# A position bias turned by DMA, and an output bias added by VectorE

## The reference

```
proj = x @ w_in[l]
a_glu, q, k, v, q_idx, k_idx, w_idx = jnp.split(proj, SPLITS, axis=-1)
conv_out = conv_group(a_glu, ...)                 # GLU, causal conv(31), LN, silu
# attention, one block of 128 queries:
score = jnp.einsum('bths,bth->bts', relu(q_idx . k_idx), w_idx)
_, sel = lax.top_k(causal score, 64)
dist = q_pos - sel
logits = q . k[sel] * scale + rel_bias[rel_bucket(dist)]
att_out = softmax(logits) @ v[sel]
mix = jnp.concatenate([conv_out, att_out], axis=-1) @ w_out[l] + b_out[l]
x = layer_norm(ALPHA * x + mix, ln1_g[l], ln1_b[l])
y = peer(x, ...)                                  # 128 rows of u_tab and of v_tab per token
x = layer_norm(ALPHA * x + y, ln2_g[l], ln2_b[l])
```

## Time and profile before

| what | value |
|---|---|
| median of 3 runs | 1866.46 us (1864.16 to 1868.92) |
| the profiled execution: its time | 1864.74 us |
| its span | 1862.8 us |
| busy PE, DVE, POOL, ACT | 81%, 64%, 44%, 16% |
| DMA queues, 640 us to the end | full, about 420 GB/s |

### The profile page before, as it was taken

One profiled execution on the slowest core, in us unless ns is written; L12 is line 12 of the kernel. 1 busy time (PEld: TensorE's weight loads), 2 busy tenths in 40 slices (PEclk: granted clock), 3 DMA queues, 4 the chain that ended last, 5 costly groups with the idle time before them and its releaser, 6 DMA issues.

```text
span 1862.8 us, 17122 instructions
## 1 busy us (share of the span) xinstructions
PE 1511.3 (81%) x5812; PEld 907.7 (49%) x5812; DVE 1188.7 (64%) x2028; ACT 303.7 (16%) x428; POOL 823.1 (44%) x681
## 2 busy tenths in 40 slices
PE   8999999999996868767777766887766777876777
PEld 7899799877993323323333322333322333322333
DVE  4699998545699765756646575744655444555445
ACT  4533354534331000000000000000000000000000
POOL 0000000003884756556555555465456555556552
PEclk9999999999996989888888888898888888887889
DMA  7355443454557899999999999999999999999996
GB/s 267 136 181 185 177 149 126 163 197 180 200 192 308 336 423 422 422 422 422 421 422 422 421 421 422 408 423 422 422 422 422 422 422 422 422 422 422 421 422 276
DMA packets 91101, 633.76 MB, mean 340 GB/s; under 512 B 10354, under 2 KB 13106, under 8 KB 14642
## 3 DMA queue, kind: packets, MB, share of 16 engines
q0 software_dynamic: 74464, 542.16, 70.3%
q1 hardware_dynamic: 13828, 88.76, 13.1%
q10 hardware_dynamic: 2768, 2.33, 0.4%
HBM read 631.08 MB, written 2.12 MB: 340 GB/s over the span
## 4 chain that ended last, share of the span: by engine, by line
PE 42%; DMA 29%; DVE 18%; issue 5%; POOL 4%; ACT 1%; POOLq 0%; SPq 0%; DVEq 0%; ACTq 0%
PE psum L659 27%; DMA v_row<-in_v_tab,eslot_v 23%; DMA u_row<-in_u_tab,eslot_u 5%; PE psum L414 4%; PE psum L415 4%; PE psum L416 4%; DVE scratch L990 4%; DVE w_lo L935 3%; POOL v_row L342 2%; DVE u_row L1233 2%; POOL u_row L342 1%; DVE scratch L1185 1%; PE psum L537 1%; DVE scratch L1156 1%; DVE scratch L1200 1%
## 5 line engine op out<-in xcount | busy, mean ns | idle before, releaser
L659 PE MATMUL psum<-v_row,scratch 128*128 128x512 f32 x2032 | 945.7, 629 | 314.1 <-DMA v_row<-in_v_tab,eslot_v 227.6
L1233 DVE CUSTOM_DVE_ANT_0 u_row<-u_row,x 128x2048 f32<-128x2048 f32 x256 | 585.0, 2308 | 513.9 <-DMA u_row<-in_u_tab,eslot_u 507.3
L659 PEld LDWEIGHTS psum<-v_row,scratch 128*128 128x128 f32 x2032 | 408.2, 203 | 851.9 <-issue 569.9
L342 POOL DMA_INDIRECT v_row<-in_v_tab,eslot_v x256 | 404.2, 1579 | 113.7 <-issue 61.8
L342 POOL DMA_INDIRECT u_row<-in_u_tab,eslot_u x248 | 263.2, 1061 | 108.5 <-issue 58.0
L414 PE MATMUL psum<-xT_hi,w_hi 128*128 128x256 f32 x896 | 258.3, 288 | 10.1 <-POOL w_lo L307 4.8
L415 PE MATMUL psum<-xT_lo,w_hi 128*128 128x256 f32 x896 | 254.8, 284 | 0.0
L416 PE MATMUL psum<-xT_hi,w_lo 128*128 128x256 f32 x896 | 254.6, 284 | 0.0
L884 ACT ACTIVATE gel<-dots 128x4 f32<-128x4 f32 x64 | 13.1, 205 | 1187.4 <-DVE dots L1233 1164.9
L414 PEld LDWEIGHTS psum<-xT_hi,w_hi 128*128 128x128 f32 x896 | 173.0, 193 | 14.1 <-issue 7.9
L415 PEld LDWEIGHTS psum<-xT_lo,w_hi 128*128 128x128 f32 x896 | 173.2, 193 | 0.3 <-issue 0.2
(11 more groups left out here) (184 smaller groups left out, 905.4 us busy)
## 6 DMA issues: line engine op xcount, KB each, us to landing
w_raw<-in_w_stream SPq DMA_DIRECT2D x80, 1024.0 KB, 4.8
v_row<-in_v_tab,eslot_v POOLq DMA_INDIRECT x256, 20.9
u_row<-in_u_tab,eslot_u POOLq DMA_INDIRECT x248, 21.7
xT_raw<-in_xT SPq DMA_DIRECT2D x4, 512.0 KB, 6.5
skew<-dist_rows ACTq DMA_DIRECT2D x1, 2048.0 KB, 11.3
x<-in_x_tok POOLq DMA_DIRECT2D x1, 2048.0 KB, 10.1
ln_rows_sb<-in_ln_rows POOLq DMA_DIRECT2D x2, 1024.0 KB, 8.3
out_dram<-x SPq DMA_DIRECT2D x8, 256.0 KB, 4.7
```

The lines of the kernel that those rows point to most:

```text
L342: pool.indirect_dma_start(dst, None, tab, bass.IndirectOffsetOnAxis(ap=ids, axis=0)).then_inc(land, 16)
L659: last = pe.matmul(ps[4 * i + n][:, :], diag[k][:, j, :], v_ring[k * G + j][:, n * 512:(n + 1) * 512], start=False, stop=True, skip_group_ ...
L1233: return dve.tensor_tensor_reduce(u_ring[s], u_ring[s], x1[:, i, :], 1.0, 0.0, ALU.mult, ALU.add, dst)
```

## The change

The rows of the bias are turned by a DMA. POOL, behind the index stage (`w_used` at 8), stores `dist_row` to DRAM 128 times, each copy shifted by minus one element (2 MB in pieces of 1 KB, read from the 16 partitions of `dist_row`), waits for that to land, and loads the result as `bias` (2 MB in pieces of 1 KB). Both stand ahead of its two `cut`s. The eight products by `flip`, the eight copies by ACT, the store and the load that ACT issued, and `flip` itself are gone; DVE waits for the load (`bias_in`) where it waited for the copies. For the output, POOL loads b_out into all 128 partitions (`b_all`, 1 MB in place of 8 KB), DVE forms ALPHA * x + b_all once for each half of the tokens, and adds the bank to it; the products with ones are gone, and the last product of a unit raises `mix_done`.

```diff
+            pool.wait_ge(w_used, U_GLU)
+            pool.wait_ge(row_copied, 1)
+            pool.dma_start(turned_rows, bass.AP(tensor=dist_row, offset=P - 1, ap=[[SKEW, NH], [-1, P], [1, S]])).then_inc(row_out, 16)
+            pool.wait_ge(row_out, 16)
+            pool.wait_ge(x_split, 4)
+            pool.dma_start(bias, turned_rows.rearrange("h p s -> p h s")).then_inc(bias_in, 16)
+
             cut(scored, acc, FILL)
             cut(masked, mask, NEG)
 
             pool.wait_ge(w_used, U_OUT)
-            pool.dma_start(b_row, b_out).then_inc(b_in, 16)
+            pool.dma_start(b_all, b_out.to_broadcast([P, D])).then_inc(b_in, 16)
...
-            pe.wait_ge(skew_in, 16)
-            pe.wait_ge(pool_const, 2)
-            for n in range(8):
-                pe.wait_ge(bias_copied, max(n - 1, 0))
-                pe.matmul(ps[6 + n % 2][:, :], flip[:, :], skew[:, 2 * n:2 * n + 2, :].rearrange("p h s -> p (h s)"),
-                          start=True, stop=True).then_inc(flip_done, 1)
...
                     for i in tiles:
                         last = exact(ps[bank + i], [t[:, 4 * q + c, i * P:(i + 1) * P] for t in (cat_h, cat_l)],
-                                     [t[:, c, :] for t in w], m + c == 0, False)
+                                     [t[:, c, :] for t in w], m + c == 0, m + c == 6)
+                        if m + c == 6 and i == 0:
+                            last.then_inc(mix_done, 1)
...
-                    pe.matmul(ps[bank + i], ones_row[:, :], b_row[:, n * 512:(n + 1) * 512], start=False, stop=True).then_inc(mix_done, 1)
...
-            act.wait_ge(row_copied, 1)
-            act.dma_start(row_scratch, dist_row[:, :]).then_inc(row_out, 16)
...
-                if u == 2:
-                    act.wait_ge(row_out, 16)
-                    act.dma_start(skew, bass.AP(tensor=row_scratch.tensor, offset=0, ap=[[1, P], [SKEW, NH], [1, S]])).then_inc(skew_in, 16)
...
-            for n in range(8):
-                act.wait_ge(flip_done, n + 1)
-                act.activation(bias[:, 2 * n:2 * n + 2, :].rearrange("p h s -> p (h s)"), ps[6 + n % 2][:, :], ACT.Copy).then_inc(bias_copied, 1)
...
-                    dve.wait_ge(bias_copied, 8)
+                    dve.wait_ge(bias_in, 16)
...
                 if n == 0:
                     dve.wait_ge(row_in, 16)
+                    dve.wait_ge(b_in, 16)
+                    for i in range(TI):
+                        last = dve.scalar_tensor_tensor(out=x1[:, i, :], in0=x1[:, i, :], scalar=ALPHA, in1=b_all,
+                                                        op0=ALU.mult, op1=ALU.add)
+                    link(last)
                 for i in range(TI):
                     x_n = x1[:, i, n * 512:(n + 1) * 512]
-                    dve.wait_ge(mix_done, TI * n + i + 1)
-                    dve.scalar_tensor_tensor(out=x_n, in0=x_n, scalar=ALPHA, in1=ps[(6 if n % 2 else 0) + i][:, :],
-                                             op0=ALU.mult, op1=ALU.add).then_inc(mix_read, 1)
+                    if i == 0:
+                        dve.wait_ge(mix_done, n + 1)
+                    else:
+                        dve.wait_ge(w_used, U_OUT + RING * (n + 1))
+                    dve.tensor_tensor(x_n, x_n, ps[(6 if n % 2 else 0) + i][:, :], ALU.add).then_inc(mix_read, 1)
```

More of the change, by code:

```diff
@@ L98, in layer @@
         xl = put("xT_lo", "x_lo", [P, KC, S], F32R)
-        b_row = put("b_row", "x_hi", [1, D])
+        b_all = put("b_all", "x_hi", [P, D])
         w_raw = [put(f"w_raw{k}", "w_lo", [P, UNIT], plus=8 * k) for k in range(RING)]
@@ L108, in layer @@
         x1c = [put(f"x1T_chunks{k}", "bias", [P, 2 * S], plus=8 + 2 * k) for k in range(4)]
-        skew = put("skew", "cat_hi", [P, NH, S])
         h_most = put("glu_sb", "cat_hi", [P, CC - 1, TAPS - 1 + S])
@@ L142, in layer @@
         ident_a = sb("ident_alpha", [P, P])
-        flip = sb("flip", [P, P])
         mean_w = sb("mean_w", [P, P])
@@ L210, in layer @@
         diag = [tmp("peer", G * P).rearrange("p (j t) -> p j t", j=G) for k in range(RG)]
-        row_scratch = nc.dram_tensor("dist_rows", (NH, SKEW), F32, kind="Internal").ap()
+        turned_rows = nc.dram_tensor("turned_rows", (NH, P, S), F32, kind="Internal").ap()
         x_split = sem("x_split")
@@ L225, in layer @@
         w_in = [sem(f"w_in{k}") for k in range(RING)]
-        row_out, skew_in = sem("row_out"), sem("skew_in")
+        row_out, bias_in = sem("row_out"), sem("bias_in")
         out_done = sem("out_done")
@@ L234, in layer @@
         qidx_copied, score_done, relu_done, idx_added = (sem(n) for n in ("qidx_copied", "score_done", "relu_done", "idx_added"))
-        row_done, row_copied, flip_done, bias_copied = (sem(n) for n in ("row_done", "row_copied", "flip_done", "bias_copied"))
+        row_done, row_copied = sem("row_done"), sem("row_copied")
         scored, masked = sem("scored"), sem("masked")
@@ L291, in _ @@
             pool.memset(ident_a[:, :], 0.0)
-            pool.memset(flip[:, :], 0.0)
             pool.memset(mean_w[:, :], 1.0 / DC)
@@ L300, in _ @@
             pool.affine_select(out=ident_a[:, :], in_=ident_a[:, :], compare_op=ALU.not_equal, fill=ALPHA,
-                               base=0, pattern=[[-1, P]], channel_multiplier=1)
-            pool.affine_select(out=flip[:, :], in_=flip[:, :], compare_op=ALU.not_equal, fill=1.0,
-                               base=-(P - 1), pattern=[[1, P]], channel_multiplier=1).then_inc(pool_const, 1)
+                               base=0, pattern=[[-1, P]], channel_multiplier=1).then_inc(pool_const, 1)
             def lower(n, u, k):
@@ L484, in _ @@
                     if k == 3:
-                        pe.wait_ge(bias_copied, 8)
+                        pe.wait_ge(row_copied, 1)
                     for half in range(2):
@@ L606, in _ @@
             for n in range(4):
-                bank = 6 if n % 2 else 0
                 pe.wait_ge(mix_read, max(n - 1, 0) * TI)
@@ L613, in _ @@
                         mix(n, m)
-                pe.wait_ge(b_in, 16)
-                for i in range(TI):
-                    if n == 3:
+                if n == 3:
+                    for i in range(TI):
                         mix(n, RING - 1, (i,))
-                    pe.matmul(ps[bank + i], ones_row[:, :], b_row[:, n * 512:(n + 1) * 512], start=False, stop=True).then_inc(mix_done, 1)
             for m in range(KC // 2):
@@ L1009, in _ @@
                 if j == 2:
-                    dve.wait_ge(flip_done, 8)
                     dve.memset(h_most[:, :, 0:TAPS - 1], 0.0)
```

## The result

The changed kernel takes 1871.14 us in the median (1867.91 to 1873.48, 20 runs); the kernel before, run beside it, 1867.19 us (1862.05 to 1870.02, 20 runs). The ratio is 1.0024 with a 95% interval of 1.0017 to 1.0031, which is +4.5 us (3.2 to 5.8): a small loss, inside the 0.3% that the prediction calls no change; it said 1869.4. The profiled execution has a span of 1868.2 us, 5.4 more than before.

The account below looks back on a forecast made before the run. The bound was taken as DVE from 95 us, PE from 376 to 450, DMA queues from 640. 22.9 + 2.8 - 22.8 = +2.9 us on 1864.7 gives 1867.6; the median, 1.7 higher, 1869.4; range 1855 to 1880.

Parts of the forecast that it names:

- What bounds the kernel: First part: PE up to 81 us, DVE from 95, with 1.2 us of weight waits to 345; DMA queues from 640.
- The output products: Output stage, 376 to 450 us: dropping the products with ones gains 8.65 us (bounds 7.85 and 8.65).
- The cover of the wide pair: Output stage: DVE's two wide instructions, 4.6 us, are hidden before PE needs unit 54, with 1.8 us to spare.
- The flip: Behind the index scores: without the eight flip products PE reaches unit 8 6.3 us earlier, DVE's unit 12 at most that.
- The added wait: POOL's cuts wait for store and load: DVE's unit 12 is later by X + g - 14.15, the kernel by X + g - 22.8.
- X: Time from the 2 MB store's issue at 72.3 us to its landing: 22.9 us, bounds 11.3 and 55.7.
- g: Time that issuing the load of 2048 pieces holds POOL: 2.8 us, bounds 0.6 and 5.8.
- DVE's wait covers them: Three weight loads, 4.8 us each in the median, fall into the store's time and were claimed hidden by DVE's wait.
- The second rival: The store is slower than taken: X 30.4, g 5.8, +13.4 us, 1879.9; slower from X + g = 28.4; chance 0.23.
- The pause of PE: Between units 10 and 11 PE pauses 11 us and loses about 3 us to its clock; nothing counted.
- The first: Rival: the narrow source costs the store little, X 11.3, g 2.8; -8.7 us, 1857.8; chance 0.28.
- The third: Rival: PE bounds behind 95 us, so a late DVE costs nothing; gain 8.65 us, 1857.8; chance 0.04.

Follow-up runs that it names:

- the kernel with the DRAM source and the early copy: The changed kernel with the 16 rows first stored to DRAM, and POOL's 2 MB copy reading them there, issued near 20 us: 1854.04 us, ratio 0.9934 to before.
- the kernel that reads every eighth partition: The changed kernel with each head's row held by eight partitions, the store reading every eighth of 128: 1860.94 us, ratio 0.9973 to the kernel before.
- the two experiments that missed: The changed kernel with the first cut ahead of both DMAs, 1867.62 us, or with the store issued near 20 us, 1861.11 us; 1852 to 1854 expected of each.
- the DRAM source: The changed kernel with the 16 rows first stored to DRAM (24 KB, by ACT), where POOL's 2 MB store reads them: 1857.21 us, ratio 0.9959 to before.
- cut first: The changed kernel with POOL's first cut written ahead of its two DMAs, the source still 16 partitions: 1867.62 us, ratio 1.0010 to the kernel before.
- the wide source: POOL's 2 MB store reading the rows from DRAM; here the changed kernel with that and the first cut ahead of both DMAs: 1855.52 us, ratio 0.9946.
- the other four experiments: The kernel before with the output part alone (1857.12 us) or position part alone (1880.84); the changed kernel with first cut ahead (1867.62) or store near 20 us (1861.11).

## Why the prediction was right, and where it was not

**What bounds the kernel.** Right. The tail is untouched, DVE has nothing in which to catch up: its +14.3 at unit 13 is still +14.2 at 320 us (320.93 before, 335.14 after, the lowering behind the same convolution step).

**The output products.** 8.65 us taken, 8.4 measured in the kernel with that part alone (interval 6.0 to 10.8); by the trace of that kernel the normalisation behind the last block starts 8.47 earlier (444.08 instead of 452.55). The bounds were 7.85 and 8.65. The cover of the wide pair held, and the blocks lie 2.1 us closer: DVE's second and third reads are 21.8 us apart (410.58 and 432.34), where they were 23.9 apart (401.20 and 425.10).

**The flip.** Its 6.3 us were called the most that the stage can gain. With the wait gone, in the kernel with the DRAM source and the early copy, DVE is 4.15 us earlier at unit 12 (4.7 without the late start of that execution, 0.55 at unit 9). The 6.3 came from the side of PE and ACT alone. DVE's own list sets the rest, from the same timeline:

```profile
80.28 2.33 DVE L921 TENSOR_TENSOR w_lo<-w_raw,w_hi 128x2048 fp32r<-128x2048 f32 x1 [0.32 <-DVE scratch L938]
82.90 0.62 DVE L952 MAX8 best<-scratch 128x8 f32<-128x128 f32 x2 [0.29 <-POOL scratch L310]
```

Unit 10 begins when the scores are added up, and from there to 90.85 DVE has work, with 0.3 us of idle time. The step did not ask whether DVE could use what PE and ACT had gained.

**The added wait.** The formula, a change of X + g - 22.8, gives 25.8 + 1.2 - 22.8 = +4.2 with the measured values; measured +4.5. Its part for DVE, X + g - 14.15, gives 12.9; the trace has 14.3, of which 0.7 is a late start of the whole profiled execution (unit 9 lowered at 76.37 instead of 75.68).

**X.** 22.9 taken, 25.8 measured, between the bounds of 11.3 and 55.7. The middle by ratio came close, but had no mechanism behind it. That mechanism was there to weigh: the page's 20 us was nearer than the dist_rows row, whose one piece for each engine showed nothing of it. The reason for the upper bound, that each partition gives only its share, falls with the kernel that reads every eighth partition: 16 partitions, 13.9 us.

**g.** 2.8 taken by the slope of the earlier trace rows, 1.21 measured, and 1.24 for the first issue. 2048 pieces hold POOL 1.7 times as long as 256 did (0.73), and by the slope it would have been four times. The errors in X and g have opposite signs, +2.9 and -1.6, so the sum came out 1.3 us short of what the formula gives with the measured values. That it was so near is in part this luck.

**"DVE's wait covers them."** This sentence on the weight loads was the wrong step. It took 4.8 us each for them, from a row of loads with the engines to themselves. In the event they were starved until the store ended. In the changed kernel DVE's wait did cover them, so the time came out; but as an account of what the position part costs the step is wrong, and it led straight to the two experiments that missed. The second rival had the loads beside the store as a reason for a larger X, not as a victim.

**The pause of PE.** Cuts expected near 98, begun at 100.65; a gap of DVE of some 17, found 18.6; unit 11 done at 103.7, found 106.5 (104.21 + 2.29); unit 12 near 106, found 109.29. The three times are 2.7 us late together; 1.3 of that is X + g (27.0 for 25.7), 0.7 the late start, and the rest lies between the steps: POOL issues 0.3 later still, and goes on 0.3 behind the landing. Behind the gap the granted clock was at the lower level. Windows of the changed kernel, columns as in the earlier trace rows:

```profile
92.00:104.00 12.00, 1.40 (x12) 1.19 (x10) 2.56 (x12) 2.76 (x2) 1.86 (x3) 0.74 0.98 287
104.00:110.00 6.00, 3.44 (x16) 3.44 (x17) 5.83 (x15) 1.06 (x1) 0.00 (x0) 0.50 1.01 359
110.00:116.00 6.00, 6.00 (x47) 6.00 (x47) 5.75 (x17) 1.29 (x2) 0.00 (x0) 0.89 0.13 36
```

PE's pause is the 13.2 us of the waits view, where 11 were expected: it is done with unit 10 at 93.4 and starts again at 106.56, when unit 11 is lowered. There it is granted 0.50, the lower of the two levels (1.2 GHz of 2.4), up to 111; from 112 on it has 1.00. DVE is busy for 5.83 of the six us from 104 on: it did not wait for the slow PE, so nothing was to be counted, as said.

**The rivals.** The first (a narrow source costs little) falls with X = 25.8. What it said of a store of 11.3 us, 1857.8, is what the DRAM source gave with 11.0: 1857.2. That the match is so close is partly chance, since its g was 1.6 too large and 1.5 us are lost later, to PE's clock (last section). The third (the delay is absorbed) falls with the constant shift. The second was the right kind (the store is slower than taken), but short of its point of decision: X + g was 27.0, and it needed 28.4.

## What to carry to other kernels

Before a transfer is put beside a stream, look at which partitions it reads: one that reads from 16 neighbouring partitions kept the DMA engines 96% busy at 121 GB/s, where they move 420 in the last part of this kernel, and the other loads paid, at each of the three places tried. When a wait is long, ask what else ends with it: taking one cause away shows the next (cut first: 18.6 us for POOL became 14.1 for the weights), so a test that removes the wait alone does not measure its price. And a delay passes through a bound engine in full: 14.3 us late stayed 14.2. A lead needs a second look: 4.2 us early became 2.7, by a fall of PE's clock that a kernel without a lead had as well.

## What the runs showed of the hardware

**The narrow store and the other queue.** From 78 to 98 us the weight queue got 63 packets to the store's 481 (the DMA view of the changed kernel, above), though three loads were issued. The Trainium skill, DMA: Bandwidth & Descriptors, "Queues, rings and completion order", says that a DMA engine takes turns between its queues by whole packets. A load of 1 MB is 144 packets in the view (288 for two in the same stretch of the kernel before). With a turn for each packet of the store, some 24 in a microsecond, the loads issued at 82.1 and 87.8 would have been through by 98. The trace does not agree, as far as the profile's packets are those that the page means, which no view tells. With the wide source (325 to 527) it is much nearer. Why the narrow store gets so much more than its turns, no run here shows.

**POOL and DVE.** A small DVE instruction waits while POOL subtracts. DVE's timeline of the changed kernel, and POOL's:

```profile
454.33 1.25 DVE L1074 SCALAR_TENSOR_TENSOR minus_mean_rstd<-mv,rstd 128x1 f32<-128x1 f32 x1
```

```profile
450.98 4.58 POOL L302 TENSOR_TENSOR w_lo<-w_raw,w_hi 128x2048 fp32r<-128x2048 f32 x1 [0.98 <-ACT w_hi L704]
```

The same instruction took 0.16 us before; now its end falls together with that of POOL's, at 455.56. The other way round stands above: POOL's cut took 2.69 us beside DVE's lowering. The Trainium skill, SBUF — State Buffer, "Who interferes with whom", has the rule: the two share a pair of ports as an exclusive lock, which counts when POOL reads SBUF beside a DVE instruction with two SBUF inputs. Both rows agree. How much of that 1.1 us reaches the end was not tried.

**1.5 us lost to PE's clock.** In all three kernels with the DRAM source DVE is ahead of the kernel before by a constant amount up to the lowering near 313 us, and by 1.5 us less at the next. The waits of the early one (70 to 345 us) name the place, and before it was 2.2 us:

```profile
DVE convT L1042 <- PE psum L548: 3.7, 1, 3.7
```

The kernel with every eighth partition, which has no lead there (DVE 0.3 us late at 314 us), loses the same 1.5 us. What these four share, and the kernel before, the changed one and the other four experiments do not, is PE's granted clock behind a pause of 1.2 us in the attention. Windows of the kernel before, and of the one with the DRAM source, with the columns of the earlier trace rows:

```profile
244.00:248.00 4.00, 2.83 (x26) 2.59 (x27) 3.93 (x7) 4.00 (x11) 0.00 (x0) 1.00 0.29 80
248.00:252.00 4.00, 4.00 (x35) 3.67 (x33) 3.86 (x7) 1.98 (x2) 0.00 (x0) 1.00 0.51 211
```

```profile
244.00:248.00 4.00, 2.83 (x26) 2.26 (x25) 3.82 (x10) 4.00 (x7) 0.00 (x0) 1.00 0.45 158
248.00:252.00 4.00, 4.00 (x23) 4.00 (x23) 3.93 (x6) 0.95 (x1) 0.00 (x0) 0.57 0.26 109
```

After the same pause PE keeps the upper level in one and is granted 0.57 for four microseconds in the other, which is 1.7 us of work at full clock. So a lead is not needed for the loss. Why the clock falls in these four and not in the others, no run shows.
